# First MLP's down projection as seven half-size products summed token-major, in a two-layer decoder trunk

## What is computed

```python
def squared_relu_mlp(h, w_up, w_down):      # 512x1024 @ 1024x4096, then 512x4096 @ 4096x1024
    a = jax.nn.relu(h @ w_up)
    return (a * a) @ w_down
...
    for l in range(DEPTH):
        ...
        x = x + squared_relu_mlp(rms_norm(x, mlp_norm[l]), w_up[l], w_down[l])
        if l == N_A - 1:
            k_sh, v_sh = shared_kv(x, kv_norm, w_kv, k_norm)
```

## Time and profile before

| | |
|---|---|
| median of 3 runs | 1136.89 us (1136.84 to 1137.94) |
| profiled execution | 1138.04 us |
| its span, first to last instruction | 1136.2 us |
| mean granted TensorE clock | 0.998 of full speed |
| PE busy | 1116.9 us, 98%, 5240 matmuls |
| DVE busy | 707.4 us, 62% |
| ACT busy | 426.7 us, 38% |
| POOL busy | 76.0 us, 7% |
| HBM read and written | 102.93 MB and 2.10 MB |

### The profile page before, as it was taken

One profiled execution on the slowest core, in us unless ns is written; L12 is line 12 of the kernel. 1 busy time (PEld: TensorE's weight loads), 2 busy tenths in 40 slices (PEclk: granted clock), 3 DMA queues, 4 the chain that ended last, 5 costly groups with the idle time before them and its releaser, 6 DMA issues.

```text
span 1136.2 us, 13633 instructions
## 1 busy us (share of the span) xinstructions
PE 1116.9 (98%) x5240; PEld 919.4 (81%) x5240; DVE 707.4 (62%) x912; ACT 426.7 (38%) x639; POOL 76.0 (7%) x58
## 2 busy tenths in 40 slices
PE   9999999999999999999999999799999999999998
PEld 7788888888888888888888877677878888888887
DVE  5755555643543553555564478874669768778686
ACT  6221233321221231233442357653445345344343
POOL 0000012000000000002040021112200000000000
PEclk9999999999999999999999999999999999999999
DMA  7433333333233333333333200142313423423302
GB/s 186 94 93 105 104 93 99 88 110 103 85 93 99 91 106 92 93 93 96 101 108 102 95 19 20 38 167 74 93 56 111 140 69 112 125 74 122 101 1 75
DMA packets 169323, 105.84 MB, mean 93 GB/s; under 512 B 12592, under 2 KB 153904, under 8 KB 169264
## 3 DMA queue, kind: packets, MB, share of 16 engines
q1 hardware_dynamic: 168224, 105.03, 31.1%
q10 hardware_dynamic: 1040, 0.00, 0.1%
HBM read 102.93 MB, written 2.10 MB: 92 GB/s over the span
## 4 chain that ended last, share of the span: by engine, by line
PE 93%; DVE 3%; ACT 1%; issue 1%; DMA 1%; SPq 0%; ACTq 0%; DVEq 0%
PE ps L456 49%; PE ps L585 15%; PE ps L610 13%; PE ps L660 10%; PE ps L682 2%; PE ps L743 1%; PE ps L721 1%; DVE nmax L1371 1%; DMA kv<-in_x 1%; PE ps L733 1%; ACT w_hi L825 0%; PE ps L702 0%; PE ps L568 0%; PE ps L755 0%; PE ps L636 0%
## 5 line engine op out<-in xcount | busy, mean ns | idle before, releaser
L456 PE MATMUL ps<-h,w_hi 128*128 128x512 f32 x1152 | 356.8, 391 | 3.3 <-DVE w_lo L1142 1.6
L456 PEld LDWEIGHTS ps<-h,w_hi 128*128 128x128 f32 x1152 | 214.7, 188 | 48.5 <-DVE h L1407 1.8
L456 PE MATMUL ps<-h,w_lo 128*128 128x512 f32 x576 | 224.3, 389 | 0.0
L825 ACT ACTIVATE w_hi<-w_raw 128x1024 fp32r<-128x1024 f32 x129 | 134.8, 1052 | 159.9 <-DMA w_raw<-in_w_up 53.6
L1142 DVE TENSOR_TENSOR w_lo<-w_raw,w_hi 128x1024 fp32r<-128x1024 f32 x129 | 164.5, 1279 | 39.8 <-ACT w_hi L825 39.1
L585 PE MATMUL ps<-h,w_hi 128*128 128x512 f32 x512 | 158.3, 390 | 0.0
L456 PE MATMUL ps<-ah,w_hi 128*128 128x512 f32 x512 | 157.7, 389 | 0.0
L610 PE MATMUL ps<-w_hi,h 128*128 128x512 f32 x448 | 138.7, 389 | 0.8 <-ACT kv L1071 0.8
L456 PEld LDWEIGHTS ps<-h,w_lo 128*128 128x128 f32 x576 | 108.1, 188 | 22.7
L456 PEld LDWEIGHTS ps<-ah,w_hi 128*128 128x128 f32 x512 | 96.1, 188 | 20.0
L585 PEld LDWEIGHTS ps<-h,w_hi 128*128 128x128 f32 x512 | 95.6, 188 | 19.6
(11 more groups left out here) (137 smaller groups left out, 1295.5 us busy)
## 6 DMA issues: line engine op xcount, KB each, us to landing
w_raw<-in_w_up SPq DMA_DIRECT2D x64, 512.0 KB, 4.0
w_raw<-in_w_down SPq DMA_DIRECT2D x32, 512.0 KB, 3.7
b_raw<-in_w_down SPq DMA_DIRECT2D x32, 512.0 KB, 4.5
w_raw<-in_a_w_in SPq DMA_DIRECT2D x23, 512.0 KB, 3.7
w_raw<-in_w_kv SPq DMA_DIRECT2D x16, 512.0 KB, 3.6
w_raw<-in_a_w_out SPq DMA_DIRECT2D x8, 512.0 KB, 3.7
w_raw<-in_w_q SPq DMA_DIRECT2D x8, 512.0 KB, 3.3
w_raw<-in_w_o SPq DMA_DIRECT2D x8, 512.0 KB, 3.8
```

The lines of the kernel that those rows point to most:

```text
L456: last = nc.tensor.matmul(ps[:, bank, :], w[:, s, k * P:(k + 1) * P], src(half, k), start=(k == 0 and i == 0), stop=(k == KC - 1 and i == 2))
L825: nc.scalar.activation(w_hi[:, slot(n), :], w_raw[:, n % RAW, :], ACT.Copy).then_inc(s_whi, 1)
```

## The change

The first MLP's down projection is written as the second's is. `mlp1` and the loop version of `mlp` are gone; one `mlp(layer)` on every engine, without a hardware loop, serves both. The squares go to a new buffer `a_raw` (16 KB in each partition) and no longer to `xT` or `ah`. In the first MLP `x_tok` starts without the residual: the first product into each part is copied, the others are added. `xT` keeps the residual. At the end PE transposes the sum, chunk by chunk (`delta_T`), and DVE adds it to `xT` (`to_feature`). Product 6, the last, touches only features 0 to 511; chunks 4 to 7 are therefore transposed inside product 6 and right behind it, and chunks 0 to 3 after key/value slab 0. The key/value slabs take the features in the order `KCH`. The split of the key/value input, the squares and the sums of squares follow `to_feature`, and `norm_sums` moves from behind slab 0 to behind slab 2. The eight DMAs of the first quarter's down weights are issued among the output projection's slabs. The buffers `h1` and `h2` swap roles up to the first MLP; `s_used` counts the down products too, in place of `s_dp`.

```diff
+KK = (2, 3, 0, 1)
+KCH = (4, 5, 6, 7, 0, 1, 2, 3)
+T_BANK = (6, 7, 6, 7, 4, 5, 6, 7)
...
+        a_raw = sb("a_raw", [P, KC, T])
```

On SP:

```diff
             for m in range(KC):
+                if m == 2:
+                    for part in (0, 2, 3, 1):
+                        load_down(0, part)
                 load(S_OUT + m, cols(wout_d, m))
...
+            mlp(0)
             for n in range(16):
-                g, kk = n // 4, n % 4
+                g, kk = n // 4, KK[n % 4]
```

On POOL, in `norm(i)`:

```diff
                     pool.wait_ge(s_nst, i)
+                    if i == NORM_B:
+                        pool.wait_ge(s_xlo, PRODUCTS * NQ - 1)
```

On PE:

```diff
+            def delta_T(i):
+
+                c = KCH[i]
+                if i == 0:
+                    pe.wait_ge(s_dv, added(NQ - 1, 5, 1))
+                elif i == 4:
+                    pe.wait_ge(s_dv, added(NQ - 1, 6, 1))
+                if i in (2, 3, 6, 7):
+                    pe.wait_ge(s_dx, i - 1 if i < 4 else i - 3)
+                for t in range(TB):
+                    last = nc.tensor.transpose(ps[:, T_BANK[i], t * P:(t + 1) * P], x_tok[:, t, c * P:(c + 1) * P], ident[:])
+                last.then_inc(s_dT, 1)
...
+                    for p in range(PRODUCTS - 1):
                         down_product(q, p)
...
+                    def features_T(tb):
+                        delta_T(2 * tb)
+                        delta_T(2 * tb + 1)
+                    down_product(q, PRODUCTS - 1, features_T if q == NQ - 1 else None)
...
                 last.then_inc(s_used, 1)
                 if n == 0:
+                    for i in range(4, KC):
+                        delta_T(i)
+                if n == 2:
                     norm_sums(NORM_B)
```

On ACT:

```diff
+            def kv_chunk(i):
+
+                act.wait_ge(s_dx, i + 1)
+                chunk_hi(I_KV, KCH[i], g_kv)
+
+            def to_kv():
+                split(S_KV)
+                split(S_KV + 1)
+                kv_chunk(0)
+                kv_chunk(1)
+                square(NORM_B, 0, KCH[0])
+                square(NORM_B, 1, KCH[1])
+                kv_chunk(2)
+                kv_chunk(3)
+                split(S_KV + 2)
+                square(NORM_B, 2, KCH[2])
+                square(NORM_B, 3, KCH[3])
+                for i in range(4, KC):
+                    kv_chunk(i)
+                split(S_KV + 3)
+                for i in range(4, KC):
+                    square(NORM_B, i, KCH[i])
```

On DVE:

```diff
+                if q == 0 and p in (0, 2, 3, 6):
+                    V.tensor_copy(part, ps[:, CHAIN[p][tb], :]).then_inc(s_dv, 1)
+                else:
+                    V.tensor_tensor(part, ps[:, CHAIN[p][tb], :], part, ALU.add).then_inc(s_dv, 1)
...
+            def to_feature(i):
+
+                dve.wait_ge(s_dT, i + 1)
+                V.tensor_tensor(xT[:, KCH[i], :], ps[:, T_BANK[i], :], xT[:, KCH[i], :], ALU.add).then_inc(s_dx, 1)
+
+            def kv_chunk(i):
+                chunk_lo(I_KV, i, KCH[i], g_kv)
+
+            def first_kv():
+                split(S_KV)
+                split(S_KV + 1)
+
+            mlp(0, first_kv)
+            to_feature(0)
+            to_feature(1)
+            kv_chunk(0)
+            kv_chunk(1)
+            add_pair(NQ - 1, 6)
+            to_feature(2)
+            to_feature(3)
+            kv_chunk(2)
+            kv_chunk(3)
+            split(S_KV + 2)
+            for i in range(4, KC):
+                to_feature(i)
+            for i in range(4, KC):
+                kv_chunk(i)
+            split(S_KV + 3)
```

More of the change, by code:

```diff
@@ L80, in slot, with entry, raw, raw_up @@
     return n % RING
[L83 to L88, removed]
+def entry(q, e):
+    return BASE[q // NQ] + PER_Q * (q % NQ) + e
+def raw(n):
+    return n if n < S_KV else n - NQ * (PER_Q - 8)
+def raw_up(q, j):
+    return raw(BASE[q // NQ]) + 8 * (q % NQ) + j
+def used(n):
+    for base in BASE:
+        if base <= n < base + NQ * PER_Q:
+            e = (n - base) % PER_Q
+            return n + 2 if e >= 8 and e % 2 == 0 else n + 1
+    return n + 1
 RA, RB, RC = (4, 5), (6, 7), (2, 3)
@@ L368, in _ @@
                     for part in (0, 2, 3, 1):
-                        load_down(0, part)
+                        load_down(NQ, part)
                 load(S_WO + m, cols(wo_d, m))
[L371 to L378, removed]
+            mlp(1)
             for p in (4, 5, 1, 6):
@@ L536, in _ @@
                 dense(S_OUT + m, U_OUT + m, I_Z, m == 0)
[L538 to L561, removed]
             def tokens_T(m):
@@ L580, in up_unit @@
-                s_ = entry(q, j) % RING
+                wait_slab(entry(q, j))
+                s_ = slot(entry(q, j))
                 for k in range(KC):
-                    if v == 0:
-                        pe.wait_ge(s_lo, 8 * I_M1 + k + 1)
+                    if v == first:
+                        pe.wait_ge(s_lo, 8 * inp + k + 1)
                     for i, (w, half) in enumerate(((w_hi, 0), (w_hi, 1), (w_lo, 0))):
-                        last = nc.tensor.matmul(ps[:, v % 4, :], w[:, s_, k * P:(k + 1) * P], h1[:, half, k, :],
+                        last = nc.tensor.matmul(ps[:, v % 4, :], w[:, s_, k * P:(k + 1) * P], h_of[inp][:, half, k, :],
@@ L885, in _ @@
                     act.wait_ge(s_mix, 9 * (j + 1))
[L886 removed]
+                    nc.scalar.activation(h1[:, 0, j, :], mix[5 + j % 2], ACT.Copy).then_inc(s_hi, 1)
             for m in range(KC):
@@ L892, in _ @@
                 chunk_hi(I_M0, m, g_m0)
-                square(NORM_M0, m)
-            def mlp(layer, base, ubase, count, after):
-                def quarter(q, first=False, last=False):
-                    for j in range(8):
-                        split(base + j + AHEAD, q * 16)
-                        if first and j == 1:
-                            row_scales(count)
-                        for jj in ((0, 1) if j == 1 else () if j == 0 else (j,)):
-                            act.wait_ge(s_r, q * 8 + (32 * layer + jj + 1))
-                            nc.scalar.activation(ah[:, jj, :], mix[jj % 2], ACT.Square).then_inc(s_ahi, 1)
-                    for m in range(8):
-                        n = base + 8 + m + AHEAD
-                        if not (last and n + q * 16 >= S_END):
-                            split(n, q * 16)
-                        if last:
-                            after(m)
-                quarter(0, first=True)
-                with act.Fori(1, NQ - 1) as q:
-                    quarter(q)
-                quarter(NQ - 1, last=True)
@@ new lines, in a_hi @@
+            def a_hi(q, p, ks=slice(0, 4)):
+                if PRODUCTS * (q % NQ) + p >= 4:
+                    before = PRODUCTS * q + p - 4
+                    act.wait_ge(s_used, entry(before // PRODUCTS, 10 + 2 * (before % PRODUCTS)))
+                if p in (2, 3, 4, 5):
+                    act.wait_ge(s_ssum, 5 * q + (3, 4, 5, 1)[p - 2])
+                else:
+                    act.wait_ge(s_asq, 8 * q + (4 if p == 0 else 8 if p == 6 else 4 + ks.stop))
+                nc.scalar.activation(a_op[q // NQ][(PRODUCTS * q + p) % 4][0][:, ks, :], a_src[p][:, ks, :], ACT.Copy).then_inc(s_xhi, 1)
```

642 lines of the change are left out of this document (300 added, 342 removed).

## The result

The changed kernel takes 1118.91 us (median of four runs, 1118.90 to 1119.04) against 1136.90 us before. The ratio is 0.984, with a 95% interval of 0.983 to 0.985.

The account below looks back on a forecast made before the run. PE bounds the kernel at 0.2267 us per matmul. -21.8 + 3.7 (transposes) + 0.6 (sums of squares) + 0.1 (chunk 4) = -17.4 us, giving 1120.6 against the profiled 1138.04, or 1119.5 as median; range 1118.2 to 1122.2.

Parts of the forecast that it names:

- The count of matmuls: First MLP's down projection: 96 matmuls fewer at 0.2267 us each, 21.8 us off PE's path.
- Nothing beside PE in the four quarters: First MLP's quarters: DVE's added work costs nothing, covered by PE's 38.1 us against 33.49 us of DVE.
- The price named for a lost cover: First MLP's quarters: with the cover gone, each percent of DVE over PE would cost 0.4 us a quarter.
- Transposes: Between first MLP and keys/values: eight groups of four on PE, 8 x 0.44 + 3 x 0.05 = 3.7 us.
- The three changes of kind: PE entering and leaving transposes inside product 6, behind it and behind slab 0: 0.05 us each.
- The sums of squares: At `norm_sums` behind key/value slab 2, PE waits for POOL's last sum: 0 to 1.6 us, taken as 0.6.
- one meeting: A POOL sum coinciding with a two-SBUF-input DVE operation after the first MLP; one puts sum 7 at about 25.7 us.
- hand-over: First MLP's end to keys/values: new PE transposes 3.7 us, waits 0.6 (sums of squares) and 0.1 us (chunk 4).
- The burst: Output projection: eight early 512 KB weight DMAs ahead of slab 2 cost nothing, with 6.5 us of cover.
- The rival that makes the kernel slower: Output projection: weight DMAs at 95 GB/s delay slab 2, PE waits 29.6 us, time 1149 us; chance 3%.
- The clock: Rival: PE's granted clock falls where the first MLP meets keys/values, costing about 1.6 us, giving 1121; chance 5%.
- the wait at chunk 4: Before key/value slab 0, PE waits for DVE's split of chunk 4: nothing or a few tenths, taken as 0.1 us.

## Why the prediction was right

**The count of matmuls.** Right to the hundredth: four down parts of 38.08 us, 21.8 us less. It rested on one observation, that both MLPs run at 0.2267 us per matmul without a gap.

**Nothing beside PE in the four quarters.** Right, and the experiments say how far it holds: three more DVE operations of 1.2 us per down part cost 0.8 us in all, fourteen make the kernel slower than before. The price named for a lost cover, 0.4 us a quarter for each percent, was wrong: with seven, some 10% of DVE over PE, it gives 4 us a quarter, and an inner down part lost 0.8. DVE may run over within a down part and catch up in the next up part.

**Transposes.** 3.49 us against 3.7. The three changes of kind that I put at 0.05 us each show as 0.10 us in slab 0.

**The sums of squares.** The step was right in kind and too dear, 0.16 us and not 0.6, and that it came out so small is in part luck. POOL's last sum ended at t = 25.2 after product 6's start (536.97 - 511.73); I had 24.5 undisturbed, 25.7 with one meeting and 27 with two. PE came at 25.4, as forecast. Two meetings took place, one lengthening a sum by 1.2 us and one by 0.5, which by my schedule would have cost up to 1.6 us. But without them the last sum would have ended at about 23.5, a microsecond sooner than I had it: ACT reached squares 4 to 7 at 17.4 and not 18.2, and an undisturbed sum took 1.27 us and not 1.35. The two errors all but cancelled. The Trainium skill's rule (SBUF — State Buffer, section Who interferes with whom) is borne out by the two kernels without a hand-over: splits on DVE that take 1.42 us alone took 2.87 us beside POOL's sums, and 1.41 again when the sums were moved, and the changed kernel's own rows agree (2.45 us beside a sum).

**The burst.** The cost of nothing was right, its cover was mis-sized: slab 2 landed at 151.0, not 147.5. I counted 4.7 MB done in 13.6 us, about 350 GB/s. In truth 5.2 MB were under way, since output slab 1, issued just before the eight, belongs to them, and they took 17.5 us from its issue, about 300 GB/s. By the 370 GB/s of the experiment with four more DMAs slab 1 accounts for some 1.4 of the 3.5 us; the rest is the lower rate, whose cause no run shows. The rival that makes the kernel slower was thus nearer than written: the stall begins beyond 3 us and not 6.5.

**The clock.** No fall at the hand-over: sixteen transposes in a row (1.75 us) and 1.00 around them. The Trainium skill's remark in TensorE: Matmul & The Clock Gate, section Part 4: PE-mode transpose, that transposes don't count as busy for the clock, had no consequence here. What did lower the clock was waiting: 5.2 us idle at `norm_sums`. The price that I put on a fall, 1.6 us, was too high for the one that I took it from: the profiled execution before, which had it, was 1.1 us longer than its sister runs.

**The 0.6 us between forecast and time.** The sum was -17.4 and the measured -18.0; 0.44 us are the sums of squares, the rest the wait at chunk 4 that didn't come (0.1) and the transposes (0.1).

## What to carry to other kernels

Where one engine is busy without gaps at the same cost per instruction in two stages, the gain of porting a scheme from one to the other is a count of instructions; the risk sits in the joints. For a joint, write each engine's list with start times and look for the item with the least margin: here it was not the new chain of transposes and splits, but a side chain of sums on another engine, with nothing in hand. And before subtracting two traces, compare a stretch whose clock is full in both.

## What the runs showed of the hardware that I had not expected

**A PE wait costs more than its length when the clock falls with it.** 5.2 us of waiting at `norm_sums` cost 7.6 us in all four executions of that kernel (1126.47 to 1126.89), because PE ran at the lower of its two levels (granted 0.50, that is 1.2 GHz) for some 5 us behind it (the profiled execution shows it; the other three had the same mean clock, 0.997). With 2.4 us of waiting in the output projection, the profiled execution had a clock of 0.62 and 0.53 in the 4 us behind the wait, while another execution of the same kernel ran at a mean of 1.000 and was 2 us shorter. A wait of 1.6 us (transposes 4 to 7 ahead of slab 0) left the profiled execution at full clock.

**POOL's sums and DVE's two-operand splits lengthen each other.** Of the four last sums, 2.50, 1.27, 1.28 and 1.76 us, the longer ones stand where DVE splits; a DVE weight split of 1.23 us took 2.31 in the kernel without a hand-over and with late squares. The 2.50 us are the sum of the two alone, 1.23 + 1.27: by these lengths one ran behind the other. Which of the two is held can't be told from the rows' starts: in the changed kernel the sum is listed from 529.86 and the split from 530.00, yet the split took its usual 1.23 us and the sum was the one lengthened.
